# A decoder layer on one core: gates, branch projections and merge computed channel by channel, with GpSimd making the first of two additions

## The reference, cut to what matters

```python
up = jnp.einsum('bsnc,ncd->bsnd', branches, w_branch[l])
g = jax.nn.sigmoid(gate.reshape(B, S, N_BRANCH, D) + b_gate[l].reshape(N_BRANCH, D))
mixed = jnp.sum(g * up, axis=2) @ w_out[l]
h = layer_norm(DEEPNORM_ALPHA * h + mixed, ln1_g[l], ln1_b[l])
moe = hier_moe(h, router_g[l], router_g_b[l], router_e[l], router_e_b[l],
               expert_w_gate[l], expert_w_up[l], expert_w_down[l])
h = layer_norm(DEEPNORM_ALPHA * h + moe, ln2_g[l], ln2_b[l])
```

## Time and profile before

| | |
|---|---|
| median of 3 runs | 497.06 us (496.78 to 672.07) |
| profiled execution | 497.06 us, its span 495.3 us |
| PE, DVE, ACT, POOL busy | 93%, 51%, 32%, 16% of the span |
| granted TensorE clock, mean | 0.980 |
| moved by DMA | 140.84 MB |

### The profile page before, as it was taken

The page is one execution under the profiler, slowest core; times in us unless marked ns, Lnnn a source line. Parts: engine busy times, 40 slices in busy tenths (PEclk is TensorE's granted clock), DMA queues, the critical chain, the costliest instruction groups (busy, mean ns, idle before and its releaser), DMA issues.

```text
span 495.3 us, 6108 instructions
## 1 busy us (share of the span) xinstructions
PE 458.8 (93%) x2390; PEld 292.1 (59%) x2390; DVE 252.9 (51%) x493; ACT 158.8 (32%) x242; POOL 81.6 (16%) x76
## 2 busy tenths in 40 slices
PE   7999999999999999899679999999999999897880
PEld 7889998777777777778554334443353334432330
DVE  6079979978876857775571223222222221131237
ACT  3177373446553693610452001101040001000020
POOL 8865900000000004870700000000000000000000
PEclk9999999999999999999879999999999999999996
DMA  8990444444434369079956999999999999999922
GB/s 262 294 366 21 163 171 169 171 169 147 164 130 143 102 253 337 1 315 408 411 225 210 414 409 409 409 410 408 411 408 411 409 411 409 409 411 409 410 101 85
DMA packets 51417, 140.84 MB, mean 284 GB/s; under 512 B 6673, under 2 KB 10906, under 8 KB 51393
## 3 DMA queue, kind: packets, MB, share of 16 engines
q1 hardware_dynamic: 49856, 137.67, 73.1%
q10 hardware_dynamic: 1056, 2.65, 1.5%
q0 software_dynamic: 480, 0.20, 0.3%
HBM read 139.46 MB, written 1.05 MB: 284 GB/s over the span
## 4 chain that ended last, share of the span: by engine, by line
PE 59%; SPq 24%; DVE 7%; DMA 5%; ACT 3%; issue 2%; POOL 1%; DVEq 0%; ACTq 0%; POOLq 0%
SPq L450 24%; PE bank L1090 16%; PE bank L1349 9%; PE bank L996 6%; PE bank L1372 4%; PE bank L1236 4%; DMA ring<-in_expert_w_down_dram 4%; PE bank L967 4%; PE bank L1216 3%; PE bank L1287 2%; PE bank L1297 1%; PE bank L1009 1%; PE bank L1083 1%; PE bank L1021 1%; PE bank L945 1%
## 5 line engine op out<-in xcount | busy, mean ns | idle before, releaser
L1349 PE MATMUL bank<-ring,gates 128*64 128x512 f32 x512 | 115.0, 600 | 6.6 <-DMA ring<-in_expert_w_up_dram 4.4
L1090 PE MATMUL bank<-rounded 128*128 128x512 f32 x384 | 91.6, 394 | 0.0
L1090 PEld LDWEIGHTS bank<-rounded 128*128 128x128 f32 x384 | 70.8, 188 | 18.0 <-issue 4.0
L1349 PEld LDWEIGHTS bank<-ring,gates 128*64 128x64 f32 x512 | 35.8, 138 | 77.2 <-issue 65.9
L1372 PE MATMUL bank<-ring,gates 128*64 128x512 f32 x256 | 58.2, 598 | 1.2 <-DMA ring<-in_expert_w_down_dram 1.2
L1899 DVE SCALAR_TENSOR_TENSOR gates<-gates,bank 128x512 f32<-128x512 f32 x8 | 6.0, 748 | 81.5 <-PE bank L1349 81.5
L1513 DVE TENSOR_TENSOR rounded<-ring,rounded 128x1024 fp32r<-128x1024 f32 x32 | 37.0, 1222 | 13.3 <-ACT rounded L717 13.3
L1910 DVE TENSOR_TENSOR rounded<-bank,rounded 128x512 fp32r<-128x512 f32 x16 | 11.1, 692 | 53.5 <-ACT rounded L913 42.2
L1372 PEld LDWEIGHTS bank<-ring,gates 128*64 128x64 f32 x256 | 17.0, 136 | 35.3 <-issue 28.7
L717 ACT ACTIVATE rounded<-ring 128x1024 fp32r<-128x1024 f32 x32 | 31.2, 1053 | 4.5 <-PE bank L996 4.4
L996 PE MATMUL bank<-rounded 128*128 128x256 f32 x240 | 29.6, 284 | 0.0
(11 more groups left out here) (258 smaller groups left out, 562.5 us busy)
## 6 DMA issues: line engine op xcount, KB each, us to landing
ring<-in_expert_w_up_dram SPq DMA_DIRECT2D x32, 1024.0 KB, 18.2
ring<-in_expert_w_down_dram SPq DMA_DIRECT2D x32, 1024.0 KB, 18.4
ring<-in_expert_w_gate_dram SPq DMA_DIRECT2D x32, 1024.0 KB, 17.6
ring<-in_w_in_dram SPq DMA_DIRECT2D x10, 2048.0 KB, 7.9
ring<-in_w_branch_dram SPq DMA_DIRECT2D x2, 2048.0 KB, 7.9
ring<-in_w_out_dram SPq DMA_DIRECT2D x2, 2048.0 KB, 10.4
ring<-in_w_in_dram SPq DMA_DIRECT2D x3, 1024.0 KB, 13.7
ring<-in_w_in_dram SPq DMA_DIRECT2D x1, 1280.0 KB, 9.2
```

Of the source, the lines that this page charges most:

```text
L1090: last = pe.matmul(bank[:, b, :], hT_part[hpart][:, k, b * P:(b + 1) * P], w[wpart][:, k, :], start=False, stop=(k == KC - 1 and hpart == 1))
L1349: last = pe.matmul(bank[CAP * e:CAP * e + CAP, part // 2, :], xg[:, FC * h + k, c:c + CAP], w[:, e, k // 2, k % 2 * HALF:(k % 2 + 1) * HAL ...
```

## The change

- Gates by channel. `gate(t, b)` now takes the weights as the stationary operand and moves the 256 tokens: two channel chunks of 128, each 24 matmuls of 256 columns. The result has channels on the partitions, so the bias is a column (`vcol`, turned by one more small transpose at the start) that ACT adds in `gate_out`, in two operations of 128x256 instead of one of 128x512. The bias matmul and its preparation on POOL, ACT and DVE go.
- Branches by channel. `up(c)` computes 128 output channels of all four branches and all tokens: 24 matmuls of 256 columns, into two banks. DVE multiplies them (128x1024) into the gates' own place.
- Merge in place. POOL adds 128x512 (branches 0, 1 plus 2, 3), DVE adds 128x256 (`merged_sum`), ACT rounds it (`merged_rounded`), DVE subtracts (`merged_rest`). The four `turn_merged` groups of transposes go, since the sum is already by channel.
- Output product by chunks. `out_part(c, t)` uses one chunk of 128 channels for both output halves into banks 4 to 7. Its parts for c = 0 and 1 stand between up(5), up(6) and up(7); chunks 4 to 7 come last, first for token block 0, then for block 1. `residual` follows in that order.
- The second half of w_branch gets a place of its own for its high part (`rounded[RING + 3]`, over `work` and `ln1p`), and ACT rounds it ahead of the Silu of the convolution branch. DVE subtracts it ahead of the copy of that branch.
- Expert parts 0 to 7 go to slots 5, 6, 7, 2, 1, 3, 0, 4. Part 0 is issued right behind w_out, parts 1 and 2 after the branches are split, part 3 after up(7), the first halves of the last four after `out_part(3, 1)`, the second halves after `s_o` 4. The transfers of ln1's gain and bias move from ACT's queue to SP's, behind part 3. POOL clears the expert loop's first operands after dispatch instead of after the merge.

The diff, cut to its core:

```diff
@@ POOL
-                    for pair in range(NB // 2):
-                        i += 2
-                        pool.wait_ge(s_mixp, i)
-                        if pair == 0:
-                            pool.tensor_tensor(o, gated[0][:, 0], gated[0][:, 1], ALU.add).then_inc(s_mix, 2)
-                        else:
-                            link(pool.tensor_tensor(gated[1][:, 0], gated[1][:, 0], gated[1][:, 1], ALU.add))
-                            pool.tensor_tensor(o, o, gated[1][:, 0], ALU.add).then_inc(s_mix, 2)
+            for c in range(KC):
+                g = gated(c)
+                pool.wait_ge(s_mixp, c + 1)
+                pool.tensor_tensor(g[:, 0:2], g[:, 0:2], g[:, 2:4], ALU.add).then_inc(s_mixa, 1)
@@ ACT
+            for c in range(KC):
+                merged_rounded(c)
+                if 2 <= c < 6:
+                    act.wait_ge(*USED["wb0"])
+                    w_out_rounded(c - 2)
@@ PE, gate(t, b)
-                for k in range(KC):
-                    for hpart, wpart in PRODUCTS:
-                        last = pe.matmul(bank[:, b, :], hT_part[hpart][:, k, b * P:(b + 1) * P],
-                                         w[wpart][:, k, :], start=False,
-                                         stop=(k == KC - 1 and hpart == 1))
+                for c in range(2):
+                    at = (2 * b + c) * P
+                    for k in range(KC):
+                        for hpart, wpart in PRODUCTS:
+                            last = pe.matmul(bank[:, b, c * T:(c + 1) * T], w[wpart][:, k, at:at + P],
+                                             hT_part[hpart][:, k, :], start=(k == 0 and hpart == wpart),
+                                             stop=(k == KC - 1 and hpart == 1))
@@ PE, merge
+            def up(c):
+                at = 2 * ((c + 1) % 2)
+                if c == 1:
+                    pe.wait_ge(s_gsig[1], 8)
+                if c >= 2:
+                    pe.wait_ge(s_mixp, c - 1)
+                for n in range(NB):
+                    if c % 4 == 0:
+                        pe.wait_ge(s_wblo[dq], n + 1)
+                        pe.wait_ge(s_brlo, NB if n == 3 else NB - 1)
...
+            def out_part(c, t):
+                for j in range(2):
+                    pe.wait_ge(s_mTlo, c + 1)
+                    pe.wait_ge(s_wolo, c // 2 * 2 + j + 1)
...
+            for c in range(6):
+                up(c)
+            out_part(0, 0)
+            up(6)
+            out_part(1, 0)
+            up(7)
+            out_part(0, 1)
+            out_part(2, 0)
+            out_part(1, 1)
+            out_part(3, 0)
+            out_part(2, 1)
+            out_part(3, 1)
+            for t in range(TB):
+                for c in range(4, KC):
+                    out_part(c, t)
@@ DVE
+            for c in range(KC):
+                dve.wait_ge(s_up, c + 1)
+                dve.tensor_tensor(g, bank[:, at:at + 2, :].rearrange("p a (n t) -> p (a n) t", n=2), g,
+                                  ALU.mult).then_inc(s_mixp, 1)
+                if c:
+                    merged_sum(c - 1)
+                if c > 1:
+                    merged_rest(c - 2)
+                if 4 <= c < 7:
+                    out_weights_rest((0, 1, 0)[c - 4], (0, 0, 1)[c - 4])
+            merged_sum(KC - 1)
+            merged_rest(KC - 2)
             out_weights_rest(1, 1)
+            merged_rest(KC - 1)
```

More of the change, by code:

```diff
@@ L444, in hybrid_trunk_kernel, with load_part @@
         PART_USED = (m_g0, m_g, m_u0, m_u, m_d0, m_y)
-        def load_part(eng, s, pair, part):
-            src = expert_part(pair, part)
-            for e in range(2):
+        def load_part(eng, n, halves=range(2)):
+            s = EXPERT_SLOT[n % RING]
+            src = expert_part(*divmod(n, 6))
+            for e in halves:
                 eng.dma_start(expert_slot(s)[:, e], src[:, e]).then_inc(s_slot[s], 8 * 2)
@@ L836, in _ @@
             gate_out(7, 0)
+            loaded(act, "wb1")
             act.wait_ge(s_lg, 2 * TB)
             act.wait_ge(s_pT, 3 * TB)
[L839 to L840 removed]
+            for q in range(4):
+                c = slice(q * QUARTER, (q + 1) * QUARTER)
+                act.activation(rounded[WB_PART[1][0]][:, c], ring[:, SLOT["wb1"], c], ACT.Copy)\
+                    .then_inc(s_wbhi, 1)
             act.wait_ge(s_czT, 1)
@@ L1206, in out_part @@
-            def out_part(j, t, k0, k1):
-                if k0 == 0:
-                    pe.wait_ge(s_mixp, 13 + 2 * t + j)
-                w = [rounded_slot(i) for i in WO_PART[j]]
-                for k in range(k0, k1):
-                    if k % 2 == 0:
-                        pe.wait_ge(s_mTlo, k // 2 + 1)
-                        pe.wait_ge(s_wolo, 4 * (k // 4) + 2 * j + k // 2 % 2 + 1)
-                    for mpart, wpart in ((0, 0), (0, 1), (1, 0)):
-                        last = pe.matmul(bank[:, 2 * t + j, :], merged_part[mpart][:, k, t * P:(t + 1) * P],
-                                         w[wpart][:, k, :], start=(k == 0 and mpart == wpart),
-                                         stop=(k == KC - 1 and mpart == 1))
-                if k1 == KC:
-                    last.then_inc(s_o, 1)
@@ new lines, in out_part @@
+            def out_part(c, t):
+                for j in range(2):
+                    w = [rounded_slot(i) for i in WO_PART[j]]
+                    pe.wait_ge(s_mTlo, c + 1)
+                    pe.wait_ge(s_wolo, c // 2 * 2 + j + 1)
+                    for mpart, wpart in PRODUCTS:
+                        last = pe.matmul(bank[:, 4 + 2 * t + j, :], merged_part(c, mpart)[:, t * P:(t + 1) * P],
+                                         w[wpart][:, c, :], start=(c == 0 and mpart == wpart),
+                                         stop=(c == KC - 1 and mpart == 1))
+                    if c == KC - 1:
+                        last.then_inc(s_o, 1)
+                if (c, t) == (3, 1):
+                    last.then_inc(s_ohalf, 1)
```

296 lines of the change are left out of this document (99 added, 197 removed).

## The result

| | before | changed |
|---|---|---|
| median | 496.92 us (496.39 to 672.07, 4 runs) | 502.77 us (501.32 to 504.27, 4 runs) |
| ratio | | 1.0135, 95% interval 1.0114 to 1.0156 |
| profiled execution, its span | 497.06, 495.3 us | 501.32, 499.6 us |
| granted TensorE clock, mean | 0.980 | 0.972 |
| branch projections begin | 185.83 us | 180.46 us |

The changed kernel is 1.35% slower: a difference that its runs can tell from none, and less than 2%. The one execution of 672.07 us is not in the ratio. The forecast was 501.0 us, "same".

What follows compares the result with a forecast made beforehand. Bound: 40 expert parts streaming for 205 us after the loop frees its first slot, so the loop's start counts. Span 495.3 + 2.2 (later LayerNorm) + 1.7 (clock) = 499.2, plus 1.76 around it: 501.0 us; 498 to 503 (0.50), 493 to 507 (8 in 10).

Steps and rivals of the forecast that it cites:

- Gates: The 16 gates as 48 matmuls of 256 columns: 5.86 us each for 6.08, together -3.4 us.
- Stop A: PE waits before the fourth branch of up(0), behind ACT's moved rounding and the Silu: 3.6 us.
- Stop B: PE waits in out_part(0, 0) for DVE's first two pieces of w_out: 1.1 + 3.3 us.
- Stop C: PE waits in out_part(2, 0) for w_out's fourth piece, behind DVE's last chunk and POOL's addition: 3.3 us.
- POOL's addition: In the merge, POOL and DVE share when side by side: addition 1.30 us alone, 2.33 beside DVE's SBUF operations.
- The clock: One fall to half clock behind the merge's three stops, +1.7 us; none to three falls, 0 to 5.1 us.
- PE's own work: In the merge: branches 23.4 us (before 22.5), output product 22.1 as before, four transpose groups gone, -4.1 us.
- The end of the output product: End of PE's last out_part, forecast at 238.5 us, 2.5 later than the 236.0 of before.
- Hidden stops: Rival, chance 0.22: DVE, ACT and POOL keep ahead, merge stage ends 9.3 us earlier, 487.5 us.
- Clock falls: Rival, chance 0.18: the clock falls after each merge stop, 504.4 us, up to 507.
- A slow gate form: Rival, chance 0.06: gate matmuls run at the gather's 0.131 us, a gate takes 6.29 us, total 507.9.
- Earlier loads: Rival, chance 0.04: earlier expert loads move the end, up to 5 us earlier, 492 us.

Runs made afterwards that it cites:

- loads late: Changed kernel with expert parts 0 to 3 loaded only once the last merge product's weights are used, LayerNorm's parameters ahead of them: 501.54 us, ratio 1.0111.
- Silu first: Changed kernel with ACT rounding w_branch's second half after the Silu and gate_out(7, 1), DVE subtracting it behind chunk 0's multiplication: 500.35 us, ratio 1.0083.
- the edits of out_part and of the fourth piece: Two separate edits of the changed kernel: all eight branch projections before the output product, 496.89 us; w_out's fourth piece right behind the third, 497.70 us.
- the second profile: The changed kernel itself measured and profiled once more, nothing edited: 501.70 us, ratio 1.0116 to the kernel before.
- two of the experiments: "Silu first" (stop of 2.34 us), 500.35 us, and "three edits" (stop of 1.71 us), 490.24 us, both edits of the changed kernel.
- the fastest version: Changed kernel with the edits of "three edits" and both additions of a chunk on DVE, none on POOL: 486.82 us, ratio 0.9813.
- three edits: Changed kernel: Silu before rounding, DVE's four pieces split behind chunks 0 and 1; all ups before out_part; w_out's fourth piece behind its third: 490.24 us, ratio 0.9894.
- output late: Changed kernel with PE doing all eight branch projections first, then the output product: 496.89 us, ratio 1.0006.

## Why the prediction was right

It said 501.0 us; the profiled execution took 501.32 and the median is 502.77. Point by point:

- **What bounds the kernel.** Right. The end is the last landing, 210.75 us after the first freed slot (205 to 210 were forecast, so just above), and "loads late" shows that the first loads may land later at no cost. The first freed slot moved by 3.2 us and the landing by 4.3, since the stream between them took 210.75 us for 209.67 before; no run shows why.
- **Gates.** Right: gate(6, 1) ended at 168.28 us (168.6 forecast), gate(7, 1) at 180.5 (181.2). `gate_out` takes 0.84 us, not 1.02: the Silu pair, which also scales, was a price too high by 0.18.
- **Stop A**, 3.6 us forecast, 3.25 measured; "Silu first" shows its cause. **Stop B**, 1.1 + 3.3 forecast, 1.50 + 3.08 measured. **Stop C**, 3.3 forecast, 2.89 measured; the edits of out_part and of the fourth piece each removed the one they were aimed at. In sum 11.3 us forecast, 10.7 measured.
- **POOL's addition.** The step that failed is the reading of the earlier trace rows that "the rows here rather show both sharing". I priced `merged_sum` and `merged_rest` at about 0.6 each beside POOL; they took 0.41 and 1.52. In sum it is 1.9 for 1.2, 0.7 us a chunk more; on the whole chunk (2.9 us, forecast 2.4 without a piece) DVE is as slow as PE's `up` (2.93). The stops came out right by luck: the pieces were cheaper than forecast, 1.21 for 1.45, and each operation starts about 0.1 us before the end listed for the last one, so that a chunk with a piece took 4.05 us (201.25 to 205.30) for 3.9. The Trainium skill ("SBUF — State Buffer", Who interferes with whom) says that a DVE operation with both inputs in SBUF contends with a GpSimd operation that reads SBUF, and that the later one is blocked outright; `merged_rest` at 1.5 beside POOL in six chunks and 0.41 without in the other two agrees. The rows of before fit it too: POOL's 2.33 us is near its 1.30 and the 1.1 that was left of DVE's first piece, and the 3.46 us of DVE's two pieces are 2 x 1.16 and most of those 1.30.
- **The clock.** The term was mis-sized: the sum had one of the three stops followed by half clock, +1.7 us, with 0 to 5.1 as bounds. Two were in the first profile, one of them for 6.8 us instead of 3.4, and cost 4.3 us; three were in the second. The fall of the earlier trace rows behind the turned rows' wait came again (a granted clock of 0.67 from 245 to 250 us), so it moved nothing. The rule of the Trainium skill ("TensorE: Matmul & The Clock Gate", HAM oscillation — how this bites in real kernels), that each burst after a wait starts cold, was nearer than mine in the number of falls: in the second profile it holds for A, B and C, in the first for A and B. Behind the stops of 2.34 and 1.71 us in two of the experiments the clock stayed at 1.00; the page's own case has waits of about 3 to 5 us, so these are not a test of it.
- **PE's own work.** The branches' 192 matmuls at 0.122 us were right. The transposes were counted wrongly: the trace of before has 16 in the merge, two rows of 1.03 to 1.09 us, where I had four groups of 1.03. They were worth 2.1 us and not 4.1. The sum didn't use the figure, since it followed the new program in time.
- **The end of the output product** came at 241.20 us, 2.7 later than the 238.5 forecast without the clock term: half clock cost 4.3, and 0.7 came back from the last gate's earlier end, 0.6 from shorter stops and some tenths from hand-overs. With the clock term the sum had 240.2, 1.0 too little. LayerNorm took 3.98 us from there and not 4.45 (the four terms of that sum make 4.38), and the gather at the loop's start 2.71 us for 3.78, with less half clock; the stream then took 1.1 more than before, which the sum had at nothing. These errors cancel to 0.4 us of span (499.6 for 499.2), which is luck: the total is nearer than its parts. Two of the signs named in the prediction were missed by a little, this end (238 to 240 us) and the turned rows, 4.4 us later than before for 2 to 4.
- **The rivals.** Hidden stops (0.22): no. Clock falls (0.18): the mechanism was there, and its time (504.4 to 507) wasn't reached. A slow gate form (0.06): no, two gates in a row took 11.7 us. Earlier loads (0.04): later ones changed nothing, earlier ones were not tried; the first freed slot, not a load, released the stream.

Where the gain went: 4.1 us came off PE up to the last gate and 0.9 in the merge, where the transposes are gone and the branches cost more, and 5.9 us more of stops and 4.3 us of half clock took more than that back. The version without a stop over 0.54 us and without half clock, whose output product ends 9.6 us earlier than before, shows the other side.

## What to carry to other kernels

Before moving a step earlier in an engine's program, follow who waits for the step that it now precedes: 3.9 us of rounding ahead of a Silu of 1.0 us stopped the engine that sets the pace for 3.25 us, and the half clock behind it cost 2.6 more. Filling the stop with idle work was no substitute here: in the profile as much half clock came behind the next stops instead. Place an operand's last preparation by the first product that needs it, not behind the last chunk of another loop. A small addition handed to an idle engine can cost the busy one more than it saves: compare the busy engine's own times with and without the neighbour before counting the work as taken away, and measure it once the other stops are gone, since before that the effect is hidden.

## What was not expected of the hardware

- A DVE subtraction of 128x256 with both inputs in SBUF took 1.50 to 1.52 us when POOL had begun a 128x512 addition 0.2 us before it, and 0.41 us with POOL idle; POOL's took 1.40 us. When DVE's piece of 1.17 us had begun first ("three edits"), POOL took 2.20 and the pair of pieces 3.45: they take turns, whole operations at a time.
- The same stop wasn't always followed by the same fall of the clock. Behind stop C of 2.89 us there was none in one profile of the changed kernel and 3.4 us at half clock in the other; behind A 6.8 and 3.4. Over all profiles with a stop A of 3.25 us it was 6.8 us once and 3.4 six times. In the fastest version PE stood 3.11 us before the turned rows at 230.40 us, and the clock stayed at 1.00; so it did behind the same stop in "output late". What decides it wasn't tried.

```profile
230.00:235.00 5.00, 4.60 (x40) 3.97 (x40) 1.99 (x6) 3.24 (x7) 4.92 (x3) 1.00 1.03 419
```
